# Semaphores of a stage kept back for three stages, and cleared in ranges without a second meeting of the engines

## The chip, the cores and the metric

The kernel runs on one NeuronCore of a Trainium2 chip. The metric is the device time of one execution in microseconds. Before the change it is 3577.29 us, the median of three runs (3575.09 to 3577.37). Engines are named as in the profile: PE is TensorE (PEld its weight loads), DVE is VectorE, ACT is ScalarE, POOL is GpSimd, SP is SyncE. A "q" behind a name (PEldq, POOLq) marks records of the engine's sequencer: waits, semaphore instructions, issues of DMAs.

## What is computed

One inference step of a decoder trunk of two layers, all in float32, for 1024 prompt tokens and for 8 sequences of 8 new tokens each with 8192 cached ones (paged). The model width is 1024. Each layer is, cut to what matters:

```python
def hybrid_layer(x, c, pos, ckv_past, kpe_past, conv_prev, shift_prev, S0, p):
    mod = jax.nn.silu(c) @ p['w_ada'] + p['b_ada']
    shift, scale, gate = mod[:, :D_MODEL], mod[:, D_MODEL:2 * D_MODEL], mod[:, 2 * D_MODEL:]
    u = rms_norm(x, p['norm_g']) * (1.0 + scale[:, None]) + shift[:, None]
    q_a, kv_a, k_rope, z_mla, cb, cc, cx, z_conv, rw, z_rw, g_merge = split_cols(u @ p['w_in'])
    ...   # A: latent attention over the prompt, or over the page cache and the new tokens
    y_mla = (o_mla * jax.nn.silu(z_mla)) @ p['w_mla_out']
    conv_out, conv_state = causal_conv(cc * cx, conv_prev, p['conv_w'])              # B
    y_conv = (jax.nn.silu(z_conv) * cb * conv_out) @ p['w_conv_out']
    ...   # C: RWKV-7 recurrence
    y_rw = (o_rw * jax.nn.silu(z_rw)) @ p['w_rwkv_out']
    gm = jax.nn.sigmoid(g_merge)
    merged = (gm[..., :D_MODEL] * y_mla + gm[..., D_MODEL:2 * D_MODEL] * y_conv
              + gm[..., 2 * D_MODEL:] * y_rw)
    return x + gate[:, None] * (merged @ p['w_out']), ...
```

A last RMS norm follows the two layers. The new latent keys, rotary keys and states are outputs too. The change touches none of this arithmetic.

## The kernel before, in words

The kernel is one straight line of stages. Each stage is a function that opens a `Phase` (line 153) and in it one `nc.Block()`: a program for each engine, written out by hand, in which engines wait for each other on the stage's own semaphores. The order is: start; then for each of two layers mla, conv, rwp (the three projections), rwkv (gates and recurrence), attn (prompt attention), dec (attention of the new tokens over the page cache), lift, merge, out; then final. Three further Phases lie around stages and have no Block of their own: rw around rwp and rwkv, page around attn and dec, and stream around everything (it holds the two semaphores of the weight ring and one more). That makes 25 Phases and 20 Blocks.

A token matrix is tiled as 8 chunks of 128 rows by 1088 columns (1024 prompt tokens and 64 new ones), the columns in thirds of 364, 364 and 360. A weight chunk (128 by 128 in 8 pieces, 512 KB) comes through a ring of two places: SyncE issues the load of chunk c + 2 when the matmuls of chunk c are done (line 549), across the borders of stages too.

At the end of a Block all engines meet: each raises a semaphore, GpSimd waits for all of them and then releases all. In the profile these records carry the line of the `with nc.Block()` (344 for start, 626 mla, 768 conv, 860 rwp, 1417 rwkv, 1907 attn, 2243 dec, 2492 lift, 2589 merge, 2687 out, 2833 final).

Behind that comes the exit of the Phase (line 174): GpSimd clears each semaphore of the Phase with an instruction of its own (line 177), and then all engines meet a second time (line 178), so that none starts the next stage before the numbers are clear. The numbers are then given back and may be used by the next stage.

Lines that are named below: 585 (matmuls of a projection), 949 (of the gates), 1950 (first matmuls of attn), 2277 and 2303 (decoding), 2713 (output projection), 549 (loads of the weight ring), 2090 (copies on GpSimd at the head of attn), 2188 (gathers of pages, issued by GpSimd).

Of the kernel before, what the change touches and what calls it, by code (L numbers as in the profile page):

```python
# [136 lines left out]
class Steps:  # L137


    def __init__(self, sem, names):  # L140
        self.sem, self.at, self.last = sem, {n: i + 1 for i, n in enumerate(names)}, 0
        assert len(self.at) == len(names)
# [7 lines left out]
        engine.wait_ge(self.sem, self.at[name])  # L150


class Phase(ExitStack):

    made = 0

    def __init__(self, nc, name):
        super().__init__()  # L160
        Phase.made += 1
        self.nc, self.name, self.sems = nc, f"{name}{Phase.made}", []

    def sb(self, name, shape, dtype=F32):
        return self.enter_context(self.nc.sbuf_tensor(f"{self.name}_{name}", shape, dtype))
# [2 lines left out]
        return self.enter_context(self.nc.psum_tensor(f"{self.name}_{name}", list(shape), F32))  # L168

    def sem(self, name):  # L170
        self.sems.append(self.enter_context(self.nc.semaphore(f"{self.name}_{name}")))
        return self.sems[-1]

    def __exit__(self, *a):
        if a[0] is None:
            for s in self.sems:
                self.nc.gpsimd.sem_clear(s)
            self.nc.all_engine_barrier(sem_only=True)  # L178
        return super().__exit__(*a)


# [313 lines left out]
class WeightStream:  # L495
# [29 lines left out]
    def attention(self, l):  # L525
        half = ROPE // 2
        w_q, w_uk, w_uv = self.rows("w_q_b", l), self.heads("w_uk", l), self.heads("w_uv", l)
        w_rope = w_q.rearrange("p k (h n) -> p k h n", n=QK)[:, :, :, NOPE:]
        rope = [(3 * part + k, None, w_rope[:, k, :, part * half:(part + 1) * half]) for part in range(2) for k in range(3)]
        rounds = [[(0, i * NOPE, w_q[:, :, (2 * r + i) * QK:(2 * r + i) * QK + NOPE]) for i in range(2)] +  # L530
                  [(3, 0, w_uk[:, :, r * P:(r + 1) * P]), (5, 0, w_uv[:, :, r * P:(r + 1) * P])] for r in range(HEADS // 2)]
        return [rope] + rounds
# [2354 lines left out]
def hybrid_decoder_step(nc, ins, outs, table_where):  # L2887

    with ExitStack() as ctx, Phase(nc, "stream") as keep:
        s = setup_shared(nc, ctx, ins, outs, table_where, ins["tables"])  # L2890
        s.stream = WeightStream(keep, s)
        s.x_stored = keep.sem("x_stored")
        start(nc, s)
        for l in range(DEPTH):
            s.layer = l
            project_mla(nc, s, l)
            project_conv(nc, s, l)
            rwkv(nc, s, l)
            attention(nc, s, l)
            with nc.sbuf_tensor(f"merged{l}", [P, KD, T], F32) as merged, nc.sbuf_tensor(f"w_out{l}", [P, KD - 1, D_MODEL], F32) as w_out:  # L2900
                w_out = [w_out[:, k, :] for k in range(KD - 1)] + [s.ckv[:].rearrange("p k t -> p (k t)")[:, 0:D_MODEL]]
                merge_branches(nc, s, l, merged, w_out)
                output_projection(nc, s, l, merged, w_out)
        final_norm(nc, s)


# [29 lines left out]
```

## Time and profile before

| | |
|---|---|
| median of three runs | 3577.29 us |
| the profiled execution | 3571.28 us |
| its span, first to last instruction | 3569.5 us |
| mean granted clock of TensorE | 0.971 |
| semaphore clears in line 177 | 317, all on GpSimd |
| meetings in line 178 | 25 |

The profile is one execution. Its span lies inside the device time of that execution, 3571.28 us, which is 6.0 us below the median. Busy time of an engine counts instructions that compute; waiting, clearing a semaphore and issuing a DMA don't count. A releaser behind an arrow is what the engine's idle time ended with: "PEq L178" is TensorE's own sequencer, released by the meeting in line 178. The granted clock is 1.00 at 2.4 GHz and 0.50 at 1.2 GHz. Times in the rows are microseconds from the span's start.

### The profile page before, as it was taken

How to read it: one execution, taken by the hardware profiler on the slowest of the kernel's cores; microseconds unless marked ns; L12 is line 12 of the kernel's file. 1: busy time of each engine (PE TensorE's matmuls, PEld its weight loads, DVE VectorE, ACT ScalarE, POOL GpSimd, SP SyncE). 2: the span in 40 equal slices, each digit the busy share in tenths (PEclk: the TensorE clock that was granted, in tenths of full speed). 3: DMA queues.
4: the chain of work that ended last, by engine and by line, in shares of the span. 5: the costliest groups of instructions: out<-in, count | busy, mean ns of one | idle time of the engine just before them, and what ended most of it. 6: DMA issues, size and time to landing. Idle time of an engine off the chain costs nothing. (4 is left out here: it accounts for less than half of the span.)

```text
span 3569.5 us, 65589 instructions
## 1 busy us (share of the span) xinstructions
PE 3405.8 (95%) x28495; PEld 2203.8 (62%) x28495; DVE 1581.1 (44%) x2959; ACT 965.0 (27%) x2048; POOL 148.1 (4%) x175
## 2 busy tenths in 40 slices
PE   7999999999989899989989999999999999998997
PEld 4666655666656677755656666656665666776665
DVE  2211044545445778744322010544553567885522
ACT  3200022333245422211122001233332553222201
POOL 1000000000000022100000000000000001220000
PEclk8999999999999899989999999999999998998998
DMA  7112111111220277576011121112112204774521
GB/s 234 39 44 56 36 46 58 55 53 54 51 79 16 105 269 268 185 263 234 17 68 33 50 56 44 46 50 57 54 50 67 54 12 184 271 271 156 183 76 56
DMA packets 250916, 356.99 MB, mean 100 GB/s; under 512 B 47395, under 2 KB 222301, under 8 KB 242054
## 3 DMA queue, kind: packets, MB, share of 16 engines
q1 hardware_dynamic: 217590, 180.49, 16.7%
q0 software_dynamic: 16400, 155.53, 11.8%
q10 hardware_dynamic: 16640, 16.78, 1.4%
q8 instruction: 226, 3.70, 0.4%
q14 instruction: 60, 0.49, 0.0%
HBM read 302.17 MB, written 48.35 MB: 98 GB/s over the span
## 5 line engine op out<-in xcount | busy, mean ns | idle before, releaser
L949 PE MATMUL rwkv_gate_bank<-u,stream_ring 128*128 128x364 f32 (+1 forms) x2304 | 792.7, 485 | 3.3 <-PEq L178 3.3
L949 PEld LDWEIGHTS rwkv_gate_bank<-u,stream_ring 128*128 128x128 f32 x2304 | 415.2, 191 | 222.0 <-issue 12.7
L585 PE MATMUL mla_b<-u,stream_ring 128*128 128x364 f32 (+1 forms) x864 | 268.7, 473 | 19.9 <-PEq L178 19.9
L585 PE MATMUL rwp_b<-u,stream_ring 128*128 128x364 f32 (+1 forms) x864 | 268.3, 473 | 4.9 <-PEq L178 4.9
L2326 PE MATMUL dec_s_bank<-u,att_q_rows 32*64 32x256 f32 x8192 | 244.1, 385 | 0.0
L585 PEld LDWEIGHTS mla_b<-u,stream_ring 128*128 128x128 f32 x864 | 165.7, 192 | 121.1 <-issue 24.3
L585 PE MATMUL conv_b<-u,stream_ring 128*128 128x364 f32 (+1 forms) x768 | 236.5, 469 | 0.0
L585 PEld LDWEIGHTS rwp_b<-u,stream_ring 128*128 128x128 f32 x864 | 165.1, 192 | 105.2 <-issue 9.2
L2713 PE MATMUL out_b<-merged,w_out 128*128 128x364 f32 (+1 forms) x672 | 214.3, 471 | 6.1 <-PEq L178 6.1
L2326 PEld LDWEIGHTS dec_s_bank<-u,att_q_rows 32*64 32x64 f32 x8192 | 188.3, 134 | 37.4 <-issue 13.2
L585 PEld LDWEIGHTS conv_b<-u,stream_ring 128*128 128x128 f32 x768 | 145.1, 190 | 86.2
L2713 PEld LDWEIGHTS out_b<-merged,w_out 128*128 128x128 f32 x672 | 128.3, 191 | 84.0 <-issue 8.0
L2382 ACT ACTIVATE page_probs<-dec_s_bank,dec_minus_top 128x1024 f32<-128x1024 f32 x64 | 71.3, 1115 | 336.7 <-DVE dec_minus_top L2419 336.7
L1989 PE MATMUL attn_s<-u 96*128 96x512 f32 (+3 forms) x384 | 147.0, 492 | 4.1 <-ACT attn_probs L2063 4.1
L963 ACT ACTIVATE rwkv_gate_stage<-rwkv_gate_bank 128x364 f32<-128x364 f32 x144 | 67.8, 471 | 295.1 <-PE rwkv_gate_bank L949 294.5
L2619 PE MATMUL merge_y<-o_mla,stream_ring 128*128 128x364 f32 (+1 forms) x384 | 129.8, 482 | 2.8 <-PEq L178 2.8
L2416 DVE TENSOR_REDUCE dec_group_top<-dec_s_bank 128x1 f32<-128x1024 f32 x64 | 78.4, 1225 | 120.9 <-PE dec_s_bank L2326 120.9
L2645 DVE TENSOR_TENSOR latents<-merge_sig,merge_y 128x364 f32<-128x364 f32 (+1 forms) x144 | 76.4, 532 | 119.9 <-PE merge_y L2619 93.2
L2619 PE MATMUL merge_y<-o_side,stream_ring 128*128 128x364 f32 (+1 forms) x384 | 124.9, 468 | 0.0
L2400 DVE STREAM_TRANSPOSE u<-dec_ckv 128x2048 f32<-128x2048 f32 x52 | 116.9, 2286 | 0.1
L1647 ACT ACTIVATE rwkv_inv_x<-rwkv_inv_t 64x128 f32<-64x128 f32 x192 | 59.1, 308 | 190.6 <-DVE rwkv_inv_t L1795 188.7
L2072 ACT ACTIVATE attn_probs_t<-attn_ring 128x512 f32<-128x512 f32 (+2 forms) x192 | 87.0, 488 | 63.8 <-PE attn_ring L1998 61.6
(537 smaller groups left out, 4599.5 us busy)
## 6 DMA issues: line engine op xcount, KB each, us to landing
stream_ring<-in_w_in_dram SPq DMA_DIRECT2D x100, 512.0 KB, 4.0
merge_sig<-gates_feature_major SPq DMA_DIRECT2D x16, 1632.0 KB, 9.5
gates_feature_major<-rwkv_gate_stage SPq DMA_DIRECT2D x96, 182.0 KB, 1.9
u<-in_w_ada_dram ACTq DMA_DIRECT2D x16, 1024.0 KB, 13.9
gates_feature_major<-rwkv_gate_stage SPq DMA_DIRECT2D x48, 180.0 KB, 2.0
w_out<-in_w_out_dram SPq DMA_DIRECT2D x14, 512.0 KB, 10.8
start_ada<-in_w_ada_dram SPq DMA_DIRECT2D x6, 1024.0 KB, 11.5
x_feature_major<-o_mla SPq DMA_DIRECT2D x2, 2176.0 KB, 9.8
```

The lines of the kernel that those rows point to most:

```text
L585: mm = pe.matmul(self.banks[j % len(self.banks)][:, 0:m], self.stream.w(c, k), s.u[:, k, t0:t0 + m], start=(k == 0), stop=(k == KD - 1))
L949: mm = pe.matmul(self.banks[j % 2][:, 0:m], self.stream.w(self.first + n, k), self.s.u[:, k, t0:t0 + m], start=(k == 0), stop=(k == KD - 1))
L963: act.activation(self.stage[j % 3][:, 0:m], self.banks[j % 2][:, 0:m], ACT.Copy).then_inc(self.emptied, 1)
L1989: mm = pe.matmul(S[a % 2][:, c:c + n], q_t[r % 2][i][0:QK, qt * P:(qt + 1) * P], k_t[r % 2][i][0:QK, c:c + n], start=True, stop=True)
L2072: act.activation(probs_t[:, a // 2 % 2, i, 4 * f * P:4 * f * P + n], R[j % 2][:, 0:n], ACT.Copy).then_inc(ring_read, 1)
L2326: mm = pe.matmul(S[64 * half:64 * half + NQ, 512 * i:512 * i + NK], q, keys, start=(cb == 0), stop=(cb == BLOCKS))
L2382: act.activation(probs[:].rearrange("p (j i k) -> p i j k", j=KH, i=4), s_view.rearrange("p i (j k) -> p i j k", j=KH), ACT.Exp, scale=ATT ...
L2400: dve.transpose(kt[a % NT][half].rearrange("p (c j k) -> p j c k", c=BLOCKS, j=KH), ckv[a % NS][:, half * HALF:(half + 1) * HALF].rearrang ...
L2416: dve.tensor_reduce(group_top[:, a:a + 1], s_view, AX.XY, ALU.max).then_inc(group_topped, 1)
L2619: mm = pe.matmul(Y[j % NY][:, 0:m], s.stream.w(first + n, k0 + k), act_in[:, k, t0:t0 + m], start=(k == 0), stop=(k == k_n - 1))
L2645: dve.tensor_tensor(prod[:, j % 3, 0:m], sig[:, n % 2, br, t0:t0 + m], Y[j % NY][:, 0:m], ALU.mult).then_inc(used, 1)
L2713: mm = pe.matmul(banks[j % NB][:, 0:m], w_out[k][:, n * P:(n + 1) * P], merged[:, k, t0:t0 + m], start=(k == 0), stop=(k == KD - 1))
```

## The change

`Phase.__exit__` no longer makes the engines meet. GpSimd still clears the Phase's semaphores, but sorts their numbers and clears each unbroken run of numbers with one instruction. The numbers are not given back at once: they are held in `self.held`, put on a list, and given back when more than three Phases stand on it, oldest first. So a number that GpSimd clears behind a stage can't be used by any of the next three Phases to close. SBUF and PSUM of the Phase are given back as before. At the very end the list is emptied. The meeting at the end of each Block is unchanged.

```diff
--- before.py
+++ after.py
@@ -150,16 +150,24 @@
         engine.wait_ge(self.sem, self.at[name])
 
 
+def clear_in_ranges(pool, sems):
+    numbers = sorted(s.num for s in sems)
+    first = [n for n in numbers if n - 1 not in numbers]
+    last = [n for n in numbers if n + 1 not in numbers]
+    for a, b in zip(first, last):
+        pool.sem_clear(range(a, b + 1))
+
+
 class Phase(ExitStack):
 
-    made = 0
+    made, retired, KEPT = 0, [], 3
 
 
 
     def __init__(self, nc, name):
         super().__init__()
         Phase.made += 1
-        self.nc, self.name, self.sems = nc, f"{name}{Phase.made}", []
+        self.nc, self.name, self.sems, self.held = nc, f"{name}{Phase.made}", [], ExitStack()
 
     def sb(self, name, shape, dtype=F32):
         return self.enter_context(self.nc.sbuf_tensor(f"{self.name}_{name}", shape, dtype))
@@ -168,14 +176,15 @@
         return self.enter_context(self.nc.psum_tensor(f"{self.name}_{name}", list(shape), F32))
 
     def sem(self, name):
-        self.sems.append(self.enter_context(self.nc.semaphore(f"{self.name}_{name}")))
+        self.sems.append(self.held.enter_context(self.nc.semaphore(f"{self.name}_{name}")))
         return self.sems[-1]
 
     def __exit__(self, *a):
         if a[0] is None:
-            for s in self.sems:
-                self.nc.gpsimd.sem_clear(s)
-            self.nc.all_engine_barrier(sem_only=True)
+            clear_in_ranges(self.nc.gpsimd, self.sems)
+            Phase.retired.append(self.held)
+            if len(Phase.retired) > Phase.KEPT:
+                Phase.retired.pop(0).close()
         return super().__exit__(*a)
 
 
@@ -2902,6 +2911,8 @@
                 merge_branches(nc, s, l, merged, w_out)
                 output_projection(nc, s, l, merged, w_out)
         final_norm(nc, s)
+    while Phase.retired:
+        Phase.retired.pop().close()
 
 
 # ---- launch: one core; inputs and outputs as the reference has them ----
```

## Rows read from the trace of the kernel before

**Rows 1.** Page, part 1: engine, busy us, share of the span, instructions.

```profile
PE 3405.8 (95%) x28495; PEld 2203.8 (62%) x28495; DVE 1581.1 (44%) x2959; ACT 965.0 (27%) x2048; POOL 148.1 (4%) x175
```

**Rows 2.** Waits of TensorE: who waited for what: us in total, times, longest us.

```profile
PE mla_b L585 <- PEq L178: 19.9, 2, 10.3
PE attn_ring L1950 <- PEq L178: 15.0, 2, 7.5
PE attn_o L2011 <- ACT attn_probs_t L2072: 13.4, 22, 0.9
```

**Rows 3.** Lines 177 and 178, whole span: ns min/median/max, first to last start.

```profile
L177 POOLq EVENT_SEMAPHORE_RANGE_CLEAR  x317: 44/44/48, 57.2 to 3569.2; - x159
...
L178 PEldq EVENT_SEMAPHORE  x50: 51/51/51, 57.3 to 3569.5; - x50
```

**Rows 4.** Source lines 344, 177, 178 around the end of the start stage.

```profile
L344 PEldq EVENT_SEMAPHORE  x1: 51/51/51, 57.2 to 57.2; - x1
...
L177 POOLq EVENT_SEMAPHORE_RANGE_CLEAR  x39: 44/44/48, 57.2 to 60.3; - x39
...
L178 PEldq EVENT_SEMAPHORE  x2: 51/51/51, 57.3 to 60.5; - x2
```

**Rows 5.** Timeline, TensorE at five borders: start, us, instruction [idle before, releaser].

```profile
60.59 2.16 PE L585 MATMUL mla_b<-u,stream_ring 128*128 128x364 f32 x3 [10.30 <-PEq L178]
...
332.81 1.72 PE L585 MATMUL rwp_b<-u,stream_ring 128*128 128x364 f32 x4 [2.47 <-PEq L178]
...
469.63 0.55 PE L949 MATMUL rwkv_gate_bank<-u,stream_ring 128*128 128x364 f32 x1 [1.65 <-PEq L178]
...
1215.92 1.14 PE L2277 MATMUL dec_s_bank<-att_q_lat,tables 32*128 32x512 f32 x8 [2.44 <-PEq L178]
...
1685.96 1.54 PE L2713 MATMUL out_b<-merged,w_out 128*128 128x360 f32 x2 [3.35 <-PEq L178]
```

**Rows 6.** Source lines 177 and 178 at the ends of mla, dec and final.

```profile
L177 POOLq EVENT_SEMAPHORE_RANGE_CLEAR  x9: 44/44/44, 206.4 to 207.0; - x9
...
L178 PEldq EVENT_SEMAPHORE  x2: 51/51/51, 206.5 to 207.2; - x2
...
L177 POOLq EVENT_SEMAPHORE_RANGE_CLEAR  x34: 44/44/44, 1519.6 to 1522.1; - x34
...
L178 PEldq EVENT_SEMAPHORE  x4: 51/51/51, 1519.7 to 1522.3; - x4
...
L178 PEldq EVENT_SEMAPHORE  x4: 51/51/51, 3568.4 to 3569.5; - x4
```

**Rows 7.** Line 549, 40 to 50 us: weight loads issued, and landing.

```profile
L549 SPq DMA_DIRECT2D stream_ring<-in_w_in_dram x2: 437/4007/7577, 40.5 to 40.9; - x2
DMA to landing us min/median/max: 13.1/13.6/14.2
```

**Rows 8.** Page, part 6: DMA issues, count, KB each, us to landing.

```profile
stream_ring<-in_w_in_dram SPq DMA_DIRECT2D x100, 512.0 KB, 4.0
gates_feature_major<-rwkv_gate_stage SPq DMA_DIRECT2D x96, 182.0 KB, 1.9
```

**Rows 9.** Waits of TensorE in decoding, 1215 to 1522 us.

```profile
PE dec_pt_bank L2303 <- DVE dec_probs_t L2465: 2.0, 1, 2.0
```

**Rows 10.** Windows: us, busy (PE PEld DVE ACT POOL), granted clock, DMA, GB/s.

```profile
333.90:337.30 3.40, 3.40 (x7) 1.84 (x6) 0.00 (x0) 0.00 (x0) 0.00 (x0) 0.50 0.92 149
337.40:340.80 3.40, 3.40 (x13) 2.13 (x12) 0.00 (x0) 0.48 (x1) 0.00 (x0) 1.00 1.06 347
469.60:473.00 3.40, 3.37 (x23) 2.35 (x24) 3.20 (x19) 0.38 (x2) 0.00 (x0) 1.00 1.04 310
987.70:992.70 5.00, 4.99 (x9) 2.83 (x10) 0.00 (x0) 0.47 (x1) 2.01 (x2) 0.50 0.55 223
1217.90:1228.20 10.30, 10.30 (x111) 8.51 (x118) 8.03 (x13) 3.54 (x8) 1.89 (x2) 0.50 0.98 387
2746.20:2750.50 4.30, 4.30 (x7) 2.48 (x8) 0.00 (x0) 0.29 (x1) 1.99 (x2) 0.50 0.64 259
```

## The prediction

> **What bounds the kernel now.** I read the page's busy times first: the matmul side of TensorE is busy 3405.8 us of 3569.5, 95%, and no other engine comes near, GpSimd least of all with 148.1 us [rows 1]. So only time in which TensorE stands, or runs at its low clock, can be given back. The view of TensorE's waits tells what it stands for: the line on top is the first matmul of the mla stage, released by the meeting in line 178, 19.9 us in two times; second is the same thing at the start of attention, 15.0 us; an ordinary wait for data (attn_o for attn_probs_t) needs 22 times to reach 13.4 us [rows 2]. Such a wait is the whole gap of the border between two stages, and only part of it belongs to the exit code. To cut it apart I read the two source lines of the exit: line 177 is 317 clears of 44 ns, all on GpSimd, line 178 is 50 records on each engine, two to a meeting, so 25 meetings [rows 3].
>
> One border in detail is the end of the start stage [rows 4]. TensorE is let go by the Block's own meeting (line 344) at 57.2. GpSimd then runs 39 clears from 57.2 to 60.3, TensorE's two records of line 178 stand at 57.3 (it arrives) and 60.5 (it is let go), and its first matmul of the next stage starts at 60.59 [rows 4, 5]. Between being let go by the Block and by line 178 lie 3.3 us in which no engine has anything to do but wait for GpSimd. The other borders look the same: 9 clears and 0.8 us at the end of mla; at the end of decoding two Phases close one behind the other (dec, then page, 34 clears and two meetings) and TensorE is held from 1519.6, where the first clear starts, to 1522.3 [rows 6].
>
> **What is removed.** For each Block end I take the time from TensorE's release there to its last release in line 178. By stage, in us: start 3.3; then mla 0.8, conv 1.1, rwp 0.6, rwkv with rw 1.7, attn 1.4, dec with page 2.8 (its release by the Block's meeting lies 0.1 ahead of the first clear), lift 0.6, merge 1.3, out 1.4, which is 11.7 for layer 0 and by the same reading 11.7 for layer 1; final with stream 1.2 (the Block's release is 0.1 ahead of the 3568.4 of the row, the last one is at 3569.5). These are 19 borders between stages, and the end; rows 4 and 6 hold the first, the second, a double one and the last. Sum 27.9 us. A second way gives nearly the same: the clears follow each other every 0.07 to 0.08 us (9 of them start within 0.6, 39 within 3.1), 317 of them are 22 to 25 us, and what is left of a border beyond its clears is 0.2 us for a meeting, 25 times 5 us: 27 to 30.
>
> **What of it is on the path.** At all 19 borders the first matmul of the next stage is released by line 178, and it follows that release within 0.1 us (60.5 and 60.59 at the first) [rows 4, 5]. Nothing else is late there, so TensorE takes up the next stage after the Block's meeting as it does now after line 178. SyncE, VectorE and ScalarE are let go at the same instants, so loads that a stage issues at its head move forward with the matmuls that need them. What doesn't move forward are transfers issued in the stage before. The tightest is the first border: the two chunks of weights were issued at 40.5 and 40.9 and landed 13.1 to 14.2 us later, thus at 53.6 to 55.1, ahead of 57.2 [rows 7]. Later chunks land about 4.0 us after issue [rows 8] and are for the chunk after next. I therefore cost no border as covered by data. For the two attention and two decode starts, where GpSimd itself has early work, see below.
>
> **What is added.** GpSimd clears by ranges. A range clear was in the trace already (its name in the profile is EVENT_SEMAPHORE_RANGE_CLEAR, here over one number each), 44 ns and a pitch of 0.07 to 0.08. How many ranges a stage needs, and whether a wide one costs more, the trace doesn't show: at least 1, at most as many as there are semaphores. Between 0.1 us and today's 0.5 to 3.1 us they run on GpSimd alone, with nobody waiting. What is queued behind them on GpSimd is its own next work: the copies of line 2090 in attention, the page gathers of line 2188 in decoding, the output in final. In the worst case (as many clears as now) this work begins when it does now, less a meeting. Even that holds nobody up, because decoding's matmuls don't wait for pages: behind the border wait, TensorE's longest in the whole stage is 2.0 us, for VectorE [rows 9]. So it costs 0 on the path, and 0 to 1 us if it turned out to matter at the two decode starts. Only at the very end the clears are the last thing: 12 numbers are 0.15 to 0.9 us; contiguous numbers are the nearer reading, I take 0.2. Keeping numbers back issues no instruction. Net of this the direct part is 27.7 us.
>
> **The clock.** The gaps also cost clock. After the 2.47 us gap at the end of conv the granted clock was 0.50, the 1.2 GHz level, from 333.9 to 337.3: 7 matmuls were begun in 3.40 us where the 3.40 us after them hold 13 [rows 5, 10]. After the 1.65 us gap ahead of the gates the clock stayed at 1.00 [rows 5, 10]. The change leaves 2.47 - 1.1 = 1.4 us of the first, less than the gap that did no harm, so this stretch should go: half of 3.4, 1.7 us, twice (the layers repeat) 3.4 us. At the end of merge in layer 0 a gap of 3.35 us shrinks to 2.1, between harmless and harmful; I take half of 1.7, 0.8 us. At the head of decoding 2.44 us shrinks to 1.1, but behind it the low level lasted 10.30 us with light matmuls, partly paced by VectorE's transposes [rows 5, 10]. Bounds are 0 and half of 10.3 for each layer, thus 0 and 10.3 us; I take 0, since the work there keeps TensorE lightly used with or without the gap. The long gaps (10.30 us at the first border, 7.5 at attention) [rows 2, 5] remain long enough to lower the clock, and its return moves with the work. Clock part: 4.2 us.
>
> The page "TensorE: Matmul & The Clock Gate" of the Trainium skill, section "Part 1: The HAM clock gate", says that the activity monitor runs free of the kernel, so that where a change of level falls depends on alignment. By that rule a border gap may or may not cost at the same length; the rows agree in that the same attention start was followed by 5.0 us of low clock in one layer and 4.3 us in the other [rows 10].
>
> **Sum.** 27.7 + 4.2 = 31.9 us off the profiled execution's 3571.3 us gives 3539.4. That execution was 6.0 us below the median of the runs shown (3577.3), so against the median: 3545.4 us, 0.9% faster.
>
> **Rivals.**
> (a) The direct part comes, the clock part doesn't, because the low stretches move to other borders instead of going: 27.7 alone, 3549.6 us; with four new stretches of 1.7 us, 3556. For it: gaps of 1.4 to 2.1 us remain at many borders. Against: the gap of 1.65 us was not followed by a low clock [rows 5, 10].
> (b) Other waits take the place of the removed ones. If data or GpSimd's early work held the first border (3.3), both attention starts (3.4) and both decode starts (2.8), and the clock part (4.2) failed too, 13.7 us of 31.9 are lost: 3559.1 us. Against: the landing times above, and the immediate start of TensorE behind every release.
> (c) Slower. The 0.6 to 3.3 us of standing may be what hides the fetching of the next stage's instructions. If after the change each of the 19 borders showed a fetch of 2.0 us, about the shortest transfer from issue to landing among the large groups of the page (1.9) [rows 8], TensorE would be held 38 us instead of 26.7, and the end would save its 1.0: 11.3 - 1.0 = 10.3 us more than before, 3587.6 us. It decides from a fetch of 27.7 / 19 = 1.5 us at each border. Against: in the trace the record of line 178 stands 0.1 us behind the Block's release, and the next stage's first instruction is executed 0.1 us behind the other release; straight-line code has been running through without stops for fetching all along. "Runtime: NRT & Kernel Launch" of the Trainium skill, section "Instruction fetch mechanics", holds that the sequencer streams instructions in ahead of use, which speaks against this rival too; no row here shows the fetch itself.
> (d) The change doesn't do what it says: the kept numbers lie so scattered that ranges are single numbers. Then 12 clears stay at the end, 0.7 us, and GpSimd's work begins a little later: 3546.1 us, not to be told from the forecast. The meeting, not the form of the clears, is what holds TensorE.
>
> **How the numbers follow.** Forecast (direct part and some clock, own range 3537 to 3551) 0.72; (a) 0.12; (b) 0.10; (c) 0.03; (d) 0.03. The range takes in (a) up to its four new stretches and at the low end the decode bound, 3545.4 - 10.3 = 3535: 3535 to 3557 us. It leaves out (b) and (c) and a little of each side. A measurement of this kernel can tell some 0.2%, 7 us, from no change. Faster by more than that needs less than 3570: forecast, (a), (d) and nearly all of (b), 0.95. Within 0.2% 0.03, the far end of (b). Slower 0.02, most of (c).
>
> **What would show it.** In the profile of the changed kernel line 178's records are gone and GpSimd has few clears to a stage. TensorE's first matmul of a stage stands 0.1 us behind the Block's release, with gaps of about 7.0 us (first), 0.8 (conv), 1.4 (rwp), 1.0 (gates), 5.8 (attention), 1.1 (decode), 1.0 (lift). The clock at the head of rwp is 1.00. TensorE's busy time falls by about 4 us, the span by about 32. I am wrong if new names stand as releasers at these first matmuls, if the gaps are longer than the lengths given, or if low clock shows at borders where it was not.

## The result, and the profile after

The changed kernel takes 3526.94 us (median of four runs, 3525.47 to 3533.54); the kernel before, run beside it, takes 3576.19 us. The ratio is 0.9869 with a 95% interval from 0.9858 to 0.9881, so 1.3% faster. The forecast was 3545.4 us, the range 3535 to 3557: the direction is right, the gain is 49 us instead of 32, and the time lies 8 us below the range. In the two profiled executions the span went from 3569.5 to 3523.6 us, 45.9 us less.

The page of the changed kernel, span and busy time by engine:

```profile
span 3523.6 us, 65059 instructions
PE 3387.0 (96%) x28495; PEld 2193.9 (62%) x28495; DVE 1580.7 (45%) x2959; ACT 964.4 (27%) x2048; POOL 147.7 (4%) x175
```

TensorE's busy time fell from 3405.8 us [rows 1] to 3387.0, by 18.8 us, with the same 28495 instructions. The change removes no matmul. So besides standing less, TensorE did the same work faster.

TensorE's waits (who waited for what: us in total, times, longest), which answer to [rows 2]:

```profile
PE attn_o L2020 <- ACT attn_probs_t L2081: 13.4, 22, 0.9
PE attn_ring L1959 <- PEq L1426: 11.6, 2, 5.8
...
PE mla_b L594 <- PEq L353: 7.4, 1, 7.4
```

The wait for data (attn_o) is what it was, 13.4 us. What is left at attention's head, 11.6 us instead of 15.0, and ahead of mla, is released by the Block's own meeting (line 1426 is now `with nc.Block()` of rwkv, line 353 that of start).

The first matmul of a stage at the ends of start, mla, conv, rwp, attn and dec (start, us, instruction, idle time before it and its releaser), against [rows 5]:

```profile
56.14 2.16 PE L594 MATMUL mla_b<-u,stream_ring 128*128 128x364 f32 x3 [7.41 <-PEq L353]
...
202.65 0.41 PE L726 MATMUL conv_lat<-tables,latents 128*128 128x128 f32 x2 [0.84 <-PEq L635]
...
327.09 1.16 PE L594 MATMUL rwp_b<-u,stream_ring 128*128 128x364 f32 x3 [1.42 <-PEq L777]
...
461.57 1.46 PE L958 MATMUL rwkv_gate_bank<-u,stream_ring 128*128 128x364 f32 x4 [1.00 <-PEq L869]
...
1201.74 1.14 PE L2286 MATMUL dec_s_bank<-att_q_lat,tables 32*128 32x512 f32 x8 [1.06 <-PEq L1916]
...
1502.34 0.36 PE L2510 MATMUL lift_small<-att_top_all,tables 128*128 128x8 f32 x2 [0.99 <-PEq L2252]
```

The gaps are 7.41, 0.84, 1.42, 1.00, 1.06 and 0.99 us; the prediction gave 7.0, 0.8, 1.4, 1.0, 1.1 and 1.0. (The first is 0.4 us longer than given; that part lies ahead of the Block's release, inside the start stage.) At all 19 borders the first matmul stands 0.11 us behind the release by the Block. From the same reading the standing between that release and the first matmul was 28.8 us in all before and is 2.0 us now, 26.7 us less at the borders; with 1.0 us at the end the direct part is 27.7 us, as forecast.

The clears (line 158, on GpSimd): all of them, then the ones behind start, behind attn and at the end (count, ns min/median/max, first to last start):

```profile
L158 POOLq EVENT_SEMAPHORE_RANGE_CLEAR  x37: 44/68/247, 56.1 to 3523.6; - x37
...
L158 POOLq EVENT_SEMAPHORE_RANGE_CLEAR  x1: 247/247/247, 56.1 to 56.1; - x1
...
L158 POOLq EVENT_SEMAPHORE_RANGE_CLEAR  x1: 131/131/131, 1201.7 to 1201.7; - x1
...
L158 POOLq EVENT_SEMAPHORE_RANGE_CLEAR  x3: 45/46/73, 3523.4 to 3523.6; - x3
```

37 range clears stand in the place of 317. The one behind start covers 39 numbers and takes 247 ns, the one behind attn 17 numbers in 131 ns. Nobody waits for them except at the very end, where three are left.

So 45.9 - 27.7 = 18.2 us are left, where the prediction had 4.2 for the clock. Of these, 1.1 us fell in the start stage, ahead of anything that the change touches (that stage took 55.8 to 57.5 us in the 17 profiles of all runs); 17.1 us fell behind it. They go with the clock: the trace holds 210 us at the low level before and 154 us after. In the profile of before the low stretches that I had read were those behind borders. Others lie inside stages. This is rwkv in the kernel before: the whole stage in layer 0, two stretches of it, the whole stage in layer 1 (stretch, us, busy time and count of PE, PEld, DVE, ACT, POOL, granted clock, DMA share, GB/s):

```profile
469.00:985.90 516.90, 503.34 (x4330) 309.75 (x4330) 257.27 (x569) 156.27 (x353) 0.00 (x0) 0.99 0.20 55
504.60:508.00 3.40, 3.40 (x22) 1.82 (x20) 0.93 (x6) 0.00 (x0) 0.00 (x0) 0.50 0.00 0
518.20:525.00 6.80, 6.12 (x18) 4.08 (x19) 1.66 (x4) 1.81 (x3) 0.00 (x0) 0.50 0.00 0
2226.70:2744.40 517.70, 504.80 (x4330) 311.15 (x4330) 257.38 (x569) 156.27 (x353) 0.00 (x0) 0.99 0.20 55
```

And after; the two short stretches cover the same part of the work, from 35 to 52 us behind the start of the stage:

```profile
461.60:973.40 511.80, 498.77 (x4331) 307.23 (x4331) 257.31 (x569) 156.15 (x353) 0.00 (x0) 1.00 0.20 56
496.40:499.80 3.40, 3.40 (x70) 2.66 (x70) 2.18 (x8) 0.00 (x0) 0.00 (x0) 1.00 0.00 0
500.00:513.60 13.60, 10.63 (x57) 5.78 (x58) 9.81 (x17) 3.26 (x4) 0.00 (x0) 1.00 0.01 1
2199.70:2713.20 513.50, 500.46 (x4330) 308.12 (x4330) 257.28 (x569) 156.09 (x353) 0.00 (x0) 0.99 0.20 55
```

Behind its first matmul the stage took 516.3 and 517.0 us before and 511.7 and 513.6 after, and it has no border inside. Between 496.4 and 499.8 TensorE began 70 matmuls, nearly all of them small, at a clock of 1.00; the kernel before, at the same point of the work, began 22 in an equally long stretch at 0.50. The other stages whose length changed by over 0.5 us beside their heads are rwp (136.0 to 134.4, twice), dec (303.6 to 300.5 and 302.0 to 300.7), final (30.9 to 29.0), start (57.2 to 56.0), merge (by -0.6 in layer 1), and mla in layer 0 and attn in layer 0, which grew by 0.6 and 1.5 us.

Two of these stages answer to terms of the prediction. In decoding of layer 0 a second low stretch follows the one at the head [rows 10]. It is the first line here; then the two stretches of the changed kernel:

```profile
1235.00:1245.20 10.20, 9.43 (x97) 5.71 (x103) 7.64 (x5) 2.97 (x5) 1.08 (x2) 0.50 0.65 223
```

```profile
1204.40:1214.70 10.30, 10.30 (x127) 8.57 (x133) 8.46 (x11) 2.85 (x7) 1.26 (x2) 0.50 0.93 388
1221.50:1228.40 6.90, 6.13 (x47) 3.66 (x53) 6.90 (x4) 2.63 (x5) 0.94 (x1) 0.51 0.51 159
```

The stretch at the head is as long as it was, 10.3 us, in both layers. The second went from 10.2 to 6.9 us, in both layers. And the first matmul of out in layer 0, behind merge, with the stretch that follows it:

```profile
1664.04 1.15 PE L2722 MATMUL out_b<-merged,w_out 128*128 128x360 f32 x3 [2.11 <-PEq L2598]
...
1665.30:1668.70 3.40, 3.40 (x7) 2.01 (x6) 0.00 (x0) 0.00 (x0) 0.00 (x0) 0.50 0.96 318
```

Behind the gap of 2.11 us, where the prediction had counted on a gain of 0.8 us, there still are 3.4 us of low clock; out took 130.9 us, against 130.7 before.

### The profile page after: what moved, and what is told of

The parts are those of the page before. It is cut to its first block and busy times, and to the rows that moved or that the text cites. A ratio compares the mean times of both kernels' runs of the same rounds, so it can differ in the third digit from the quotient of the medians.

```text
span 3523.6 us, 65059 instructions
## 1 busy us (share of the span) xinstructions
PE 3387.0 (96%) x28495; PEld 2193.9 (62%) x28495; DVE 1580.7 (45%) x2959; ACT 964.4 (27%) x2048; POOL 147.7 (4%) x175
```

## The experiments

Two theories stood at first. Theory A: low clock in a stage is decided by where the light stretches and gaps of the stage's work lie in time, so anything that shifts the work changes it. Theory B: the second meeting itself lowers the clock in the stage behind it. "Stage time" below is the time from the Block's release ahead of the stage to its own, less the time to the stage's first matmul, both read from the records of the Block lines and the timeline.

### The second meeting put back; single clears

```diff
+++ meet_ranges
             clear_in_ranges(self.nc.gpsimd, self.sems)
+            self.nc.all_engine_barrier(sem_only=True)
+++ single_clears
-            clear_in_ranges(self.nc.gpsimd, self.sems)
+            for s in self.sems:
+                self.nc.gpsimd.sem_clear(s)
```

> The changed kernel with the second meeting put back behind the range clears. What is left of each border is a meeting (0.2 us) and one to three range clears (0.07 us each), so TensorE stands 0.3 to 0.4 us longer at 19 borders than in the changed kernel: 6 to 8 us. Theory A (the clock stretches fall or don't by where the gaps inside the stages happen to lie in time): 3533 to 3535 us for the direct part, and up to 8 us to either side of that from the clock. Theory B (the clock part beyond the forecast was caused by the exit code itself, through its length): directly 3534 us, and within 2 us of it, because nearly all of the standing is still gone.

> The changed kernel with one clear for each semaphore instead of ranges, still without the second meeting. Both theories: TensorE starts each stage 0.1 us behind the Block's release as in the changed kernel, since the clears run on GpSimd alone; only the end is longer, by about 10 clears of 0.07 us, 0.7 us. So 3527 to 3528 us. If the clears as such mattered (through GpSimd's late start in attention and decoding), up to 6 us more.

With the meeting: 3555.6 us (ratio to before 0.9953, 0.9936 to 0.9969). It stands 0.36 us longer at a plain border, 9.0 us at all borders and 0.5 us more at the end, but is 29 us slower than the changed kernel. Both theories missed that: theory A allowed up to 3543 us and theory B up to 3536. The 19 us beyond the standing are spread over stages; in the profiles rwkv has 10.6 of them. With single clears: 3532.5 us (0.9889, 0.9872 to 0.9905), every head 0.11 us as with ranges. So the meeting holds the engines and not the form of the clears, which is rival (d)'s point. It is 5 us above 3527, as far as the expectation's third case allowed for, in which GpSimd starts late in attention and decoding. The profile speaks against that case: beside the changed kernel's repeat (below) attn took the same within 0.1 us and dec 0.9 and 0.0 us more, while mla took 0.9 and 1.5 us more and rwkv 1.1 us more in each layer. rwkv in the run with the meeting, layer 0, its low stretch, layer 1:

```profile
463.20:981.00 517.80, 504.80 (x4330) 311.16 (x4330) 257.41 (x569) 156.31 (x353) 0.00 (x0) 0.99 0.19 55
498.80:509.00 10.20, 10.20 (x92) 6.89 (x92) 7.41 (x14) 0.00 (x0) 0.00 (x0) 0.50 0.01 2
2215.50:2734.60 519.10, 506.44 (x4330) 312.10 (x4330) 257.42 (x569) 156.30 (x353) 0.00 (x0) 0.98 0.19 55
```

The stage times are 517.3 and 518.6 us. Ahead of conv in layer 1 the same profile has low clock behind a short gap, and the stage took 125.9 us instead of 124.3:

```profile
1954.77 0.41 PE L727 MATMUL conv_lat<-tables,latents 128*128 128x128 f32 x2 [1.21 <-PEq L185]
...
1956.30:1959.70 3.40, 3.40 (x7) 2.01 (x8) 0.55 (x2) 0.00 (x0) 0.00 (x0) 0.50 0.62 182
```

All three profiles with a meeting had low clock about 35 us into rwkv so far, and none without.

### Everything 1.7 us later

```diff
+++ before_late17 (in the exit)
-            for s in self.sems:
+            for s in self.sems + self.sems[:1] * (21 if self.name[:5] == "start" else 0):
+++ after_late17 (in the exit)
+            if self.name[:5] == "start":
+                for _ in range(19):
+                    self.nc.gpsimd.sem_clear(self.sems[0])
+                self.nc.all_engine_barrier(sem_only=True)
             clear_in_ranges(self.nc.gpsimd, self.sems)
```

> The kernel before, with one semaphore of the start stage cleared 21 times more, 1.7 us on GpSimd with all engines waiting, and nothing else: everything behind the start stage lies 1.7 us later. Theory B (no effect of where things lie in time): the time before plus 1.7 us, 3577.9, within 1.5 us. Theory A: the low stretches of the clock inside the stages move, come or go, and the time differs from 3577.9 by more than 3 us to either side; the gaps at the borders are as they were.

> The changed kernel with 19 more clears and one meeting at the end of the start stage, 1.7 us in which all engines wait; everything behind lies 1.7 us later. Theory B: 3526.9 plus 1.7, 3528.6 us within 1.5 us. Theory A: off that by more than 3 us, with low clock in stages where the changed kernel had none, the head of rwp excepted: there the gap is too short for it in any position, so it stays at 1.00.

Before, later: 3576.4 us (1.0003, 0.9993 to 1.0013), within theory B's bounds. After, later: 3534.2 us, 7.2 us above the changed kernel for 1.5 us of standing at the one head, by A's words. One for each; the first shift by itself settles nothing. The profile of the kernel before, shifted, shows what moved, though it is an execution of 3587.1 us, 10.6 us above the median of its kernel: conv took 127.5 us in both layers instead of 124.3, with low clock at its head, and rwp 134.4 instead of 136.0: the low stretch had gone from one stage to the next.

### More work at the head of the gates

```diff
+++ after_work5, meet_work5, before_work5 (in GateFiller.fill)
+            for _ in range(5 if j == 0 and k == 0 else 0):
+                pe.matmul(self.banks[j % 2][:, 0:m], self.stream.w(self.first + n, k), self.s.u[:, k, t0:t0 + m], start=True, stop=True)
             mm = pe.matmul(self.banks[j % 2][:, 0:m], ...
+++ after_work2, before_work2
             the same with range(2 ...)
```

> The changed kernel, with the first matmul of the gates done 5 times more at the head of rwkv in both layers (each overwrites the last; the result stays): 1.7 us more work for TensorE and no gap. It moves the light stretch 33 to 38 us into the stage against the places where the clock may change. In the three profiles without a second meeting the clock stayed at 1.00 there, in the three with one it fell to 0.50 there in both layers. Theory A (it is the place in time that decides): the low stretch appears 31 to 36 us into rwkv in one or both layers and the stage grows by 1.7 plus 3 to 5 us; the kernel takes 3534 to 3542 us. Theory B (the meeting itself lowers the clock): the stage grows by 1.7 us in each layer, 3530.5 us in all.

> The changed kernel with the second meeting put back, and the same 5 more matmuls at the head of rwkv in both layers. Theory A: the low stretch that began 34 to 36 us into rwkv goes in one or both layers, and the stage, 517 to 519 us long so far, takes 513 to 516 us although it has 1.7 us more to do; the kernel 3555.6 + 3.4 less 4 to 10: 3549 to 3555 us. Theory B: the low stretch stays, 3559 us.

> The kernel before with the same 5 more matmuls at the head of rwkv. Theory A: as with the meeting put back: low stretches at 34 to 36 us go in one or both layers; 3576.5 + 3.4 less 3 to 10: 3570 to 3577 us. Theory B: 3579.9 us with the low stretches in place.

The five matmuls took 3.0 us, not 1.7: in float32 each is two records of 0.3 us. So the shift was 3.0 us, and the expected effect in the first run did not come: rwkv grew by 3.07 and 3.00 us and kept its clock, and yet the kernel took 3538.4 us, 5.5 us above 3526.9 plus 6.0. Where these 5.5 us lie its profile can't show, because that execution took 3531.8 us. With the meeting: 3553.0 us, 2.7 us less than without the extra 6.0 us of work (the ratios to the kernel before, 0.9952 and 0.9953, are equal):

```profile
462.70:980.00 517.30, 503.49 (x4340) 310.05 (x4340) 257.19 (x569) 156.13 (x353) 0.00 (x0) 1.00 0.20 55
2214.70:2731.40 516.70, 503.44 (x4340) 309.85 (x4340) 257.17 (x569) 156.15 (x353) 0.00 (x0) 1.00 0.20 55
```

516.7 and 516.3 us with 3.0 us more to do, against 517.3 and 518.6; less 3.0 us that is 513.7 and 513.3. (Theory A had 513 to 516 us with a shift of 1.7 us.) In layer 0 there was no low clock at 35 us although the meeting was there. Theory B, by which the meeting lowers the clock at that place, is out by this. Before with the five: 3572.6 us, also no slower than without (3573.7, run beside it), and in layer 1 no low stretch at 35 us.

> The changed kernel with the first matmul of the gates done 2 times more in each layer, 0.6 us each by the 3.0 us that 5 of them took, 2.4 us in all. Theory A: this shifts the light stretch of rwkv by 1.2 us, into the places where the clock fell in the runs with a meeting (the clock may change 34.3 to 35.6 us into the stage there): rwkv is 515 to 519 us in one or both layers against 511.7 and 513.6, and the kernel 3533 to 3540 us. Without an effect of place: 3529.3, or 3534.5 from the typical 3532.

> The kernel before with 2 more matmuls at the head of the gates in each layer, 2.4 us of work. Theory A: the shift of 1.2 us moves the low stretch of rwkv away in one or both layers, 3 to 5 us each: 3571 to 3577 us. Without an effect of place: 3577.5 us.

Two more matmuls, 1.2 us a layer, in the changed kernel: 3535.7 us, 9.8 us above its repeat (below), run beside it, for 2.4 us of work. The kernel's time is in theory A's range, but not for the reason it gave: a low stretch came 34 us into the stage's own work in layer 0, yet rwkv took 514.6 and 514.8 us, not 515 to 519. By the two profiles the growth lies in mla of layer 1 (1.6 us), attn of layer 0 (1.9), dec (0.9 and 1.6), merge of layer 1 (1.1) and final (1.4). In the kernel before: 3569.7 us, 3.3 us below the 3573.0 run beside it, with more to do, though the ratio, 0.9992 (0.9980 to 1.0004), doesn't tell the two apart. Its rwkv in layer 0, conv in layer 1 and rwkv in layer 1:

```profile
468.50:989.40 520.90, 507.65 (x4334) 312.96 (x4334) 257.38 (x569) 156.15 (x353) 0.00 (x0) 0.98 0.20 55
1967.00:2095.40 128.40, 126.21 (x417) 77.75 (x417) 20.43 (x36) 11.33 (x24) 0.00 (x0) 0.97 0.17 43
2230.90:2744.70 513.80, 499.98 (x4334) 307.97 (x4334) 257.32 (x569) 156.16 (x353) 0.00 (x0) 1.00 0.20 55
```

Two runs of one and the same instruction list on TensorE in one execution: 520.2 and 513.0 us behind their first matmul, with clock 0.98 and 1.00. In layer 0 the low stretch had not moved away, as expected, but grown. Such a difference for one list is what theory A says, in one profile. Over all profiles of all runs here rwkv's stage time, less what a run added, goes by where its low clock began, counted from the first matmul of the stage's own work:

```
low clock begins (us into   stage time, us    kernels (layer)
the stage's own work)
33.7 to 34.2                518.6 to 518.9    before_late17 (0, 1), before_work2 (0), meet_ranges (1),
                                              old_exit_mla (0, 1), after_warm8 (1)
34.3 to 34.8                513.3 to 513.4    old_exit_conv (1), after_work2 (0), meet_work5 (1)
34.8 to 35.1                516.3 to 517.3    before (0, 1), before_work5 (0), meet_ranges (0)
none before 46              511.7 to 514.6    before_work5 (1), before_work2 (1), meet_work5 (0),
                                              after, after_again, single_clears, after_late17,
                                              after_work5, warm8_pad2 (0, 1), after_work2 (1),
                                              old_exit_conv (0), after_warm8 (0)
```

(after_warm is left out, its useless matmuls made the stage longer.) Kernels with a meeting ahead of rwkv and kernels without one stand in the first line, in the second and in the last. So a meeting is neither needed for low clock in rwkv nor enough for it, and shifts of 1.2 and 3.0 us were enough to bring it or to take it away. The meeting is not without weight, though: low clock began before 46 us in 9 of the 12 stages of kernels with a meeting at every border, and in 5 of the 20 others.

How long the clock is low accounts for the stage time. Over the same 32 stages, between the start and the last microseconds of the stage: no low clock 511.7 to 511.8 us (5 stages), 3.4 us of it 513.3 to 513.7 (13), 6.8 us 514.4 to 514.6 (3), 10.2 us 516.3 (2), 13.7 us 517.0 and 517.3, and 17.1 us 518.6 to 518.9 (7). Each microsecond at the low clock costs 0.4 to 0.5 us here.

### The changed kernel once more

> The changed kernel itself once more, on the chip of the other runs of this call. The variants of it that only shift it (one clear per semaphore, 1.7 us later, 5 more matmuls) come out at 3531.8 to 3532.5 us once their own additions (0.7, 1.7, 6.0 us) are taken off, 5 us above its first 3526.9. If that first number was a lucky place in time, this one is 3530 to 3533 us; if the program has a place in time of its own that it keeps, 3525 to 3529 us.

3525.9 us (0.9885, 0.9867 to 0.9904). So the first number was no chance: the median comes back. The program doesn't sit still, though. One of the four executions took 3537.6 us, and between the two profiles rwkv in layer 0 differs (511.7 and 513.4 us) and attn in layer 0 (228.3 and 226.1).

### One border with the old exit

```diff
+++ old_exit_mla; old_exit_conv with ("conv",)
+            if self.name.rstrip("0123456789") in ("mla",):
+                for s in self.sems:
+                    self.nc.gpsimd.sem_clear(s)
+                self.nc.all_engine_barrier(sem_only=True)
+            else:
                 clear_in_ranges(self.nc.gpsimd, self.sems)
```

> The changed kernel with the old exit (single clears and a second meeting) at the end of mla alone, in both layers. Directly 0.7 us longer standing at two borders, 1.4 us. If the gap ahead of conv, 1.65 us again, is what can lower the clock at conv's head (it did so in 3 profiles of kernels with the old exit, by 3.2 us in conv in 4 of their 8 layers, and never without it), conv takes 127.5 us instead of 124.3 in one or both layers in some place in time, and the kernel 3527.3 to 3534 us. If a gap of this length does nothing, as I held in the prediction, conv stays at 124.3 and the kernel takes 3527.3 us, apart from what the shift does in rwkv.

> The changed kernel with the old exit at the end of conv alone, in both layers. Directly 1.0 us at two borders, 2.0 us, and with the gap ahead of rwp back at 2.47 us the clock falls at its head: rwp 136.0 us instead of 134.4 in both layers, 3.4 us. 3525.9 + 5.4 = 3531.3 us, apart from what the shift does in rwkv. If the clock at the head of rwp has to do with the whole of the old kernel and not with this gap, rwp stays at 134.4.

The old exit behind mla alone costs 9.9 us, 3535.8 us against 3525.9, for 1.6 us of standing. The profile is the longest of its four executions, 3542.1 us. conv's first matmul and what follows it, then rwkv in both layers and its low stretch:

```profile
203.39 0.41 PE L731 MATMUL conv_lat<-tables,latents 128*128 128x128 f32 x2 [1.66 <-PEq L187]
...
204.40:207.80 3.40, 3.40 (x8) 1.98 (x8) 0.98 (x3) 0.00 (x0) 0.00 (x0) 0.50 0.58 179
207.80:211.20 3.40, 3.40 (x12) 2.09 (x11) 0.00 (x0) 0.00 (x0) 0.00 (x0) 0.99 0.03 5
463.80:982.50 518.70, 506.45 (x4330) 311.99 (x4330) 257.25 (x569) 156.13 (x353) 0.00 (x0) 0.98 0.19 55
498.00:511.70 13.70, 13.70 (x118) 8.92 (x118) 9.93 (x20) 0.00 (x0) 0.00 (x0) 0.50 0.00 1
2211.30:2730.00 518.70, 506.47 (x4330) 311.89 (x4330) 257.32 (x569) 156.14 (x353) 0.00 (x0) 0.98 0.19 55
```

A gap of 1.66 us, and the clock falls to 0.50 behind it; conv took 126.0 and 125.9 us in the two layers. (The expectation's 3.2 us in conv was seen in three of the four stages that it names; the fourth had 1.6.) My reading that a gap of this length does no harm was wrong. And rwkv, 260 us further on and with its own head at 0.11 us, took 518.6 us in both layers: the shift put it into its worst place.

The old exit behind conv alone: 3533.1 us. Here the expectation failed the other way:

```profile
328.86 1.46 PE L599 MATMUL rwp_b<-u,stream_ring 128*128 128x364 f32 x4 [2.52 <-PEq L187]
...
329.00:332.40 3.40, 3.40 (x12) 2.13 (x13) 0.00 (x0) 0.00 (x0) 0.00 (x0) 1.00 0.71 169
```

A gap of 2.52 us, and the clock stays at 1.00; rwp took 134.4 us in both layers. A gap as long as the one of [rows 5] can go unpunished. The trace of the kernel before could have told that much, at the head of out in layer 1:

```profile
3417.52 1.75 PE L2713 MATMUL out_b<-merged,w_out 128*128 128x360 f32 x5 [2.76 <-PEq L178]
...
3417.50:3420.90 3.40, 3.38 (x11) 2.19 (x12) 0.06 (x1) 0.00 (x0) 0.00 (x0) 1.00 0.64 188
```

That gap is 2.76 us and the clock stays at 1.00. In the run with everything 1.7 us later the same gap was 3.08 us, and it stayed there too.

### Useless matmuls where TensorE stands

```diff
+++ after_warm (rwkv's end; also 16 at the end of out in layer 0, and 2, 6 and 1 in lift, into a bank of their own)
                 fill()
+                pe.wait_ge(gates.emptied, len(gates.jobs) - 1)
+                for _ in range(13):
+                    pe.matmul(gates.banks[0][:, 0:THIRD], s.tab["ones"], s.u[:, 0, 0:THIRD], start=True, stop=True)
+++ after_warm8: 8 instead of 13, 8 instead of 16, in lift 1, 3 and none
+++ warm8_pad2: as after_warm8, and 2 more matmuls at the head of the gates in layer 1
```

> The changed kernel with useless matmuls where TensorE stands and waits anyway: 16 at the end of out in layer 0, 13 at the end of rwkv, 9 in lift; their results are thrown away. If the clock costs what I think, the head of mla in layer 1, of attention and of merge, and lift itself, run at 1.00: 2 + 2 times 2.5 + 2 times 6 us, about 15 to 19 us less than the changed kernel, 3508 to 3512 us. If low clock there costs nothing because other engines pace these places, 3527 us, or more where the useless matmuls are in the way.

> As the run with useless matmuls in TensorE's idle places, but so few that they end before TensorE is needed: 8 at the end of out in layer 0 (16 made that stage 5.9 us longer), 8 at the end of rwkv, 4 in lift. The gains seen there (attention 4.0 and 0.7, merge 1.1 and 1.8, mla 1.6, lift 0.7 each) stay and the losses go: 8 to 12 us less than the changed kernel of the same call, 3516 to 3522 us. If the clock were not the cause, no difference.

> The kernel with useless matmuls in TensorE's idle places, and 2 more matmuls (1.2 us) at the head of the gates in layer 1 alone, where rwkv fell into a bad place (518.7 us). Theory A: the shift by 1.2 us puts it into the best place, rwkv in layer 1 takes 511.8 to 513.6 us plus 1.2, so 4 to 6 us less than the 518.7 for 1.2 us more work; the kernel 3517 to 3519 us. Without an effect of place: 3523.5 us.

after_warm: 3529.2 us. The clock stayed up where it should, but the useless matmuls were too many: out in layer 0 grew from 130.9 to 136.8 us and rwkv by 2 to 4, which ate the expected gain of 15 to 19 us. after_warm8: 3522.3 us (0.9856, 0.9839 to 0.9873), 3.6 less than the changed kernel run beside it instead of 8 to 12. lift and rwkv, first in the changed kernel's repeat (lift and rwkv of layer 0), then with the useless matmuls (lift of layer 0, rwkv of layer 1):

```profile
1501.50:1516.70 15.20, 9.84 (x68) 9.34 (x68) 4.97 (x9) 0.21 (x1) 0.00 (x0) 0.57 0.47 181
460.90:974.40 513.50, 500.44 (x4330) 308.14 (x4330) 257.34 (x569) 156.26 (x353) 0.00 (x0) 0.99 0.20 55
```

```profile
1502.80:1513.90 11.10, 9.28 (x76) 6.51 (x76) 4.97 (x9) 0.21 (x1) 0.00 (x0) 1.00 0.64 248
2193.90:2712.80 518.90, 511.32 (x4346) 315.19 (x4346) 257.39 (x569) 156.10 (x353) 0.00 (x0) 0.98 0.19 55
```

lift went from 15.2 to 11.1 us in either layer, at a clock of 1.00 instead of 0.57. But rwkv in layer 1, shifted by all of this, was at 518.7 us. With 2 more matmuls at its head:

```profile
461.70:973.50 511.80, 503.65 (x4346) 310.26 (x4346) 257.15 (x569) 156.13 (x353) 0.00 (x0) 1.00 0.20 56
2188.40:2703.30 514.90, 506.55 (x4350) 311.93 (x4350) 257.16 (x569) 156.09 (x353) 0.00 (x0) 1.00 0.20 55
```

514.8 us with 1.2 us more to do, and the kernel 3513.1 us (0.9829, 0.9809 to 0.9850), the fastest of all, 13 us faster than the change and 60 us faster than the kernel before. rwkv in layer 1 came out as expected. How much of the kernel's 9.1 us less than after_warm8 is due to it is open: in the profiles the stage gives 4.0 us, but its first matmul already stands 5.4 us earlier (2188.6 and 2194.0 us), and nothing ahead of it was edited. One of the four executions of after_warm8 took 3512.4 us without the edit.

### What the shifts average to

Each family's medians, less what a variant added: with the old exit 3576.2, 3574.9, 3566.6 and 3567.3, mean 3571.2; with the change (the kernel, its repeat, single clears, later, 5 and 2 more matmuls) 3526.9, 3525.9, 3531.9, 3532.7, 3532.4 and 3533.3, mean 3530.5. The mean difference is 40.7 us: 27.7 direct and 13 that I put down to the clock. With four and six values that spread by 9.6 and 7.4 us, the 13 is an estimate good to some 3 us. The rest of the 49 us, 8.5 us, is that this pair compares a kernel in a poor place with one in a good place. The 13 us show in the stage times averaged over the same profiles: rwkv 516.4 and 513.3 in each layer, conv 125.7 and 124.3, rwp 135.4 and 134.4, dec 303.0 and 301.2, final 30.2 and 29.0; together 16 us, which agrees with 13 as well as four and six profiles can.

Place is not all of it. Take from each kernel its additions and the standing that it has more than the changed kernel: the four with the old exit then take 3538.9 to 3548.5 us, the two with the meeting behind range clears 3546.1 and 3537.4, and the six without a second meeting 3525.9 to 3533.3. The two sets don't overlap. So in these kernels a meeting at every border costs some 12 us on top of its standing, by the two means, and shifts alone don't account for that. Part of it are the heads of conv and rwp, where it makes the gaps longer. Why the kernels with it also come to rest in rwkv's poor places more often was not settled. What the table shows is that places recur: of the 18 stages in its last line 10 had their next low stretch at 49.2 to 49.5 us, three at 46.8 to 46.9, and five had none. Why they recur stays open too.

## Why the prediction was wrong, point by point

- **What bounds the kernel** (TensorE; its waits on the second meeting can be given back): right. The waits released by line 178 are gone, and no new name took their place.
- **Direct part, 27.7 us**: right to the tenth, with the gaps as given but for the first, which is 0.4 us longer. The borders were costed at nothing for data, and no border waited for any.
- **What is added**: right. 37 range clears run beside other work. I had left open whether a wide one costs more; it does, 247 ns for 39 numbers against 44 ns for one.
- **The clock part, 4.2 us, is the term that failed.** In its place the profiles leave 18.2 us (17.1 without the start stage), and the families some 13 us on average. Of the 18.5 us between forecast and measurement 14 are this term; the other 4.5 are the forecast's baseline, a kernel before at 3577.3 and not 3576.2 us, and an allowance of 6.0 us between profiled execution and median, which was 4.9 us before and 1.5 us after. Four steps of the clock part were wrong. First, I looked for low clock only behind the borders that the change touches, and took work inside a stage as unchanged. rwkv alone, whose instructions are the same, takes 511.7 to 518.9 us by its place, up to 7 us in each layer; it gave 4.6 and 3.4 us in the measured pair, and I had put it at nothing without a reason. Second, I took the length of a gap alone as what decides, from one harmless gap of 1.65 us and one harmful of 2.47 us. The run with the old exit behind mla has low clock behind 1.66 us, the one with the meeting behind 1.21 us, the one behind conv none behind 2.52 us. The 3.4 us for rwp did come in the measured pair (136.0 to 134.4, twice, 3.2 us), so here a right number stood on a rule that doesn't hold; it came by luck. Third, by the same rule I gave the head of out 0.8 us; its low stretch stayed and it gave none. Fourth, I gave dec 0 between bounds of 0 and 10.3, for the stretch at its head. That one did stay, but the stage gave 3.1 and 1.3 us, with a second stretch 17 us further on that went from 10.2 to 6.9 us and that I hadn't looked at.
- **The page of the Trainium skill that I cited** ("TensorE: Matmul & The Clock Gate", section "Part 1: The HAM clock gate") said that the change of level depends on alignment. The rows agreed, I wrote so, and then used it only to allow for low stretches that move to other borders, a loss. It also meant that stages far from any border could gain.
- **Rivals.** (a) had the sign of the clock's surprise the wrong way: low stretches did move, and the sum fell. (b) and (c) didn't happen; a fetch that shows would have stood at the heads, and these are 0.11 us. (d) is refuted for the ranges. Its point that the meeting and not the form of the clears holds TensorE is shown by the heads of the run with single clears, 0.11 us; that this run is 5 us slower is within what the shifts do.
- **Range.** It ended at 3535 because I added only decoding's bound. rwkv's 516.3 and 517.0 us lie 9.9 us above twice its best, 511.7; with that beside decoding's bound it would have begun at 3525, and the 3526.9 measured would lie inside.

## What to carry to other kernels

When a meeting of all engines guards only the reuse of semaphore numbers, keep the numbers back and drop it: with its clears each border cost 0.6 to 3.3 us, and the gain on the path could be read from the release times to a tenth. In this kernel, where TensorE's clock falls in many places, shifts of 1 to 3 us, even ones that add work, changed the time by several us in stages that they don't touch; a difference under some 10 us between two versions of this kernel says nothing about the edit until it is seen with two or three different shifts. Filling TensorE's idle places with useless matmuls that end in time brought 3.6 us beyond the change, and with two more that shift one stage 13 us, of which a good part can't be put down to the shift.

## What the runs showed of the hardware

- One instruction list, run for the two layers in one execution, took 520.2 and 513.0 us, with a mean granted clock of 0.98 and 1.00.
- The length of an idle gap alone doesn't tell whether the clock falls: it did behind 1.21 and 1.66 us ahead of conv and didn't behind 2.52 us ahead of rwp or 2.76 and 3.08 us ahead of out in layer 1. Behind the gaps of 0.84 and 1.42 us that the change leaves there it fell in none of the nine profiles without an old exit.
- The clock can fall without a gap, amid small matmuls: in the 14 stages of the first three lines of the table it fell among rwkv's two batches of 64 small matmul records (70 records began in the 3.40 us shown of the changed kernel, TensorE busy all the time), where the longest idle time nearby was 0.2 us.
- In rwkv each microsecond at the low clock lengthened the stage by 0.4 to 0.5 us: 511.7 us with none, 518.6 to 518.9 with 17.1 us.
- A range clear of semaphores takes 44 to 48 ns for one number and 247 ns for 39, about 5 ns more for each.
